# The opening of a two-block kernel on one Trainium2 core: modulation columns in four groups of 512, context prepared between the query slots

## What is computed

```python
s_lat, s_ctx = silu(c), silu(c_ctx)
mod_l = split(s_lat @ ada_w[0] + ada_b[0], 6)       # six vectors of 1024: shift, scale, gate, ...
a_lat = rmsnorm(x, norm1_g[0]) * (1 + mod_l[1]) + mod_l[0]
mod_c = split(s_ctx @ ada_w[0] + ada_b[0], 6)
a_ctx = rmsnorm(ctx, norm1_g[0]) * (1 + mod_c[1]) + mod_c[0]
p_lat = a_lat @ mix_w_in + mix_b_in                 # q, k, v and three hyena inputs
kv_ctx = a_ctx @ mix_w_in[:, KV] + mix_b_in[KV]     # k and v of the context
k_all, v_all = concat([k_c, rope(k_l)]), concat([v_c, v_l])
...                                                  # attention, hyena, out, MLP, second layer, second stack
```

## Time and profile before

| | |
|---|---|
| median of three runs | 2553.88 us |
| the profiled execution | 2555.92 us, its span 2554.1 us |
| TensorE / VectorE / ScalarE / POOL busy | 96% / 65% / 38% / 6% |
| granted TensorE clock, mean | 0.986 |
| DMA from 10 to 40 us | 393, 418 and 413 GB/s |
| loads in the queue up to q weights 0 | vec 251.5 KB, x 2 x 1024 KB, ctx 1024 KB, groups 0 to 3 of 2 x 768 KB, weights 1024 KB |
| landing of the two x halves, of ctx | 10.4 and 13.2 us, 16.2 us |
| q slot 0, q slot 1, k slot 0 on TensorE | from 47.09, 59.9 and 73.00 us |

### The profile page before, as it was taken

One profiled execution on the slowest core, in us unless ns is written; L12 is line 12 of the kernel. 1 busy time (PEld: TensorE's weight loads), 2 busy tenths in 40 slices (PEclk: granted clock), 3 DMA queues, 4 the chain that ended last, 5 costly groups with the idle time before them and its releaser, 6 DMA issues.

```text
span 2554.1 us, 27261 instructions
## 1 busy us (share of the span) xinstructions
PE 2463.0 (96%) x10726; PEld 1925.9 (75%) x10726; DVE 1662.7 (65%) x2162; ACT 960.8 (38%) x1280; POOL 162.3 (6%) x234
## 2 busy tenths in 40 slices
PE   6999879999999999999999999999999999999997
PEld 3876338788888888888766788888877667888886
DVE  7876678965668955668965695554699556733334
ACT  4325444422333422334843343122357343422221
POOL 0100140000000000000100000000001000000000
PEclk8999989999999999999999999999999999999999
DMA  7432003555552454553211234554522112223222
GB/s 289 175 125 75 17 17 107 178 190 204 171 203 91 160 178 165 181 169 120 83 57 52 74 104 163 179 181 151 179 101 92 54 44 66 85 87 118 92 86 78
DMA packets 66423, 315.36 MB, mean 123 GB/s; under 512 B 7127, under 2 KB 12631, under 8 KB 45304
## 3 DMA queue, kind: packets, MB, share of 16 engines
q1 hardware_dynamic: 41240, 222.39, 25.2%
q0 software_dynamic: 25056, 91.24, 10.9%
HBM read 311.50 MB, written 2.10 MB: 123 GB/s over the span
## 4 chain that ended last, share of the span: by engine, by line
PE 78%; DVE 12%; ACT 4%; issue 2%; DMA 2%; SPq 0%; POOL 0%; DVEq 0%; ACTq 0%
PE psum L677 20%; PE psum L678 20%; PE psum L679 20%; PE psum L1089 3%; PE psum L1045 2%; PE psum L845 2%; PE psum L1074 2%; PE psum L1063 1%; PE psum L1064 1%; DVE w_lo L1765 1%; PE psum L901 1%; DMA big<-in_ada_first 1%; DVE rstd L1608 1%; DVE squares L1654 1%; PE psum L804 1%
## 5 line engine op out<-in xcount | busy, mean ns | idle before, releaser
L1765 DVE TENSOR_TENSOR w_lo<-w_raw,w_hi 128x2048 fp32r<-128x2048 f32 (+1 forms) x192 | 418.8, 2181 | 323.7 <-ACT w_hi L1229 321.3
L677 PE MATMUL psum<-x_hi,w_hi 128*128 128x512 f32 x1568 | 618.1, 394 | 8.5 <-DVE w_lo L1765 5.3
L678 PE MATMUL psum<-x_lo,w_hi 128*128 128x512 f32 x1568 | 611.3, 390 | 0.0
L679 PE MATMUL psum<-x_hi,w_lo 128*128 128x512 f32 x1568 | 611.2, 390 | 0.0
L1229 ACT ACTIVATE w_hi<-w_raw 128x2048 fp32r<-128x2048 f32 (+1 forms) x192 | 350.5, 1826 | 505.0 <-DMA w_raw<-in_w 503.2
L678 PE MATMUL psum<-hidden_lo,w_hi 128*128 128x512 f32 x960 | 373.5, 389 | 0.0
L677 PEld LDWEIGHTS psum<-x_hi,w_hi 128*128 128x128 f32 x1568 | 295.1, 188 | 73.5 <-DVE w_lo L1765 7.2
L677 PE MATMUL psum<-hidden_hi,w_hi 128*128 128x512 f32 x896 | 349.1, 390 | 0.0
L679 PE MATMUL psum<-hidden_hi,w_lo 128*128 128x512 f32 x896 | 348.6, 389 | 0.0
L678 PEld LDWEIGHTS psum<-x_lo,w_hi 128*128 128x128 f32 x1568 | 295.2, 188 | 62.1 <-issue 3.1
L679 PEld LDWEIGHTS psum<-x_hi,w_lo 128*128 128x128 f32 x1568 | 295.0, 188 | 61.8
(11 more groups left out here) (438 smaller groups left out, 3251.4 us busy)
## 6 DMA issues: line engine op xcount, KB each, us to landing
w_raw<-in_w SPq DMA_DIRECT2D x160, 1024.0 KB, 4.9
ada_w<-in_ada POOLq DMA_DIRECT2D x168, 512.0 KB, 4.0
w_raw<-in_w SPq DMA_DIRECT2D x32, 704.0 KB, 4.1
big<-in_ada_first SPq DMA_DIRECT2D x12, 768.0 KB, 14.1
big<-in_ada POOLq DMA_DIRECT2D x6, 512.0 KB, 4.2
extra<-in_w_uq SPq DMA_DIRECT2D x8, 384.0 KB, 3.2
residual<-in_xT SPq DMA_DIRECT2D x2, 1024.0 KB, 9.4
cond_row<-in_c_row SPq DMA_DIRECT2D x4, 512.0 KB, 4.4
```

The lines of the kernel that those rows point to most:

```text
L677: mm(o, w_h, x_h, start=first, stop=False)
L678: mm(o, w_h, x_l, start=False, stop=False)
L679: return mm(o, w_l, x_h, start=False, stop=last)
L1765: v.tensor_tensor(wl[:, r, 0:n], raw[:, r, 0:n], wh[:, r, 0:n].bitcast(f32), ALU.subtract).then_inc(w_split.sem, 1)
```

## The change

Groups of 512 columns: four of them make the 2048 that are needed, in three buffers of 2 x 1 MB; the remaining columns become 32 instead of 30 (LATE_N), with 2, 2, 5, 5, 5, 5 in the slots of q, k and v. In the queue, x comes first, then the four groups, then q weights 0, ctx, q weights 1. The preparation of the context (squares, sum, root, product, modulation, high and low parts) is moved on all three engines: TensorE sums its squares between q slots 0 and 1, ScalarE evacuates q slot 0 before it takes the context's root, and VectorE starts on it after the low part of q weights 1. The low part of q weights 0 moves into `modulated`, behind the second tile. In the k slots, the context's matmuls follow all of the latent ones.

```diff
-ADA_COLS = 384
+ADA_COLS = 512
 ADA_N = 6 * D // ADA_COLS
-ADA_DEEP = 4
+ADA_DEEP = 3
+ADA_TILES = ADA_COLS // P
 CTX_ADA_N = -(-2 * D // ADA_COLS)
 
 MODS_N = 6 * D // P
 LATE_AT = CTX_ADA_N * ADA_COLS // P
 LATE_N = MODS_N - LATE_AT
-EARLY_N = 22
+EARLY_N = 24
...
-    for (i, s), count in zip(late, (2, 2, 4, 4, 5, 5, 2, 2, 2, 2)):
+    for (i, s), count in zip(late, (2, 2, 5, 5, 5, 5, 2, 2, 2, 2)):
...
-        first_norms = {T: (t1[:], rstd[:]), C: (big[:, 31, 0:C], staging[:, 0, 0:C])}
+        first_norms = {T: (t1[:], rstd[:]), C: (big[:, 31, 0:C], rstd[:, 0:C])}
...
-            load_first_ada(0)
             for half in range(2):
                 k4 = slice(4 * half, 4 * half + 4)
                 load(h[:, k4, :], a["xT"].rearrange("(k p) t -> p k t", p=P)[:, k4, :], "x_loaded%d" % half)
+            for n in range(CTX_ADA_N):
+                load_first_ada(n)
+            load_slot(mixed[0], 0)
             load(big[:, 0:4, :].rearrange("p a (b t) -> p (a b) t", t=C),
                  a["ctxT"].rearrange("(k p) t -> p k t", p=P), "ctx_loaded")
-            for n in range(1, ADA_DEEP):
-                load_first_ada(n)
-            load_slot(mixed[0], 0)
-            for n in range(ADA_DEEP, CTX_ADA_N):
-                load_first_ada(n)
             load_slot(mixed[0], 1)
             load(big[:, 28:30, :], a["rope1"].rearrange("b p t -> p b t"), "rope1_loaded")
+            load(cond_row[:], a["c_row"], "row_loaded")
             load(big[:, 30, :], a["v_bias"], "vbias_loaded")
-            load(cond_row[:], a["c_row"], "row_loaded")
             load_slot(mixed[1], 0)
...
-                            if st.name == "k":
-                                ins = three(B(4 + 2 * r + m, C), wh[:, b, w], wl[:, b, w], ch[:, k, :], cl[:, k, :], *ends)
                         if x_read and k < st.kt - 1:
                             ins.then_inc(x_read.sem, 1)
+                    if st.name == "k":
+                        for k in order:
+                            if s == 0:
+                                next_k(k)
+                            for m in range(st.mt):
+                                w = slice((k * st.mt + m) * P, (k * st.mt + m + 1) * P)
+                                ins = three(B(4 + 2 * r + m, C), wh[:, b, w], wl[:, b, w], ch[:, k, :], cl[:, k, :],
+                                            k == order[0], k == order[-1])
...
-                for t in range(3):
-                    ins = mm(ps[:, 6, 8 + 6 * n + 2 * t:10 + 6 * n + 2 * t], first_rows[:, n, t * P:(t + 1) * P],
+                for t in range(ADA_TILES):
+                    at = 8 + 2 * (ADA_TILES * n + t)
+                    ins = mm(ps[:, 6, at:at + 2], first_rows[:, n, t * P:(t + 1) * P],
                              V("group_sum", 0, 2), start=True, stop=True)
...
             first_ada(0)
             first_sum_of(T)
-            first_ada(1)
-            first_sum_of(C)
-            turn(0)
-            for n in range(2, CTX_ADA_N):
+            for n in range(1, CTX_ADA_N):
                 first_ada(n)
                 turn(n - 1)
             me.count(turn(CTX_ADA_N - 1).then_inc(S("ada_turned").sem, 1), S("ada_turned"))
-            products(mixed[0], xh, xl)
-            products(mixed[1], xh, xl)
+            slot(mixed[0], 0, xh, xl, next_k)
+            first_sum_of(C)
+            slot(mixed[0], 1, xh, xl)
+            products(mixed[1], xh, xl, False)
             products(mixed[2], xh, xl, False)
...
-            first_squares([ctx_in[:, k, :] for k in range(KD)], C, KD - 1, {0: "ctx_loaded"})
             first_scale(T, 6, 1)
-            row_copy(0)
-            first_scale(C, 7, 2)
-            for n in range(1, ADA_DEEP):
+            for n in range(CTX_ADA_N):
                 row_copy(n)
             split_hi(0)
-            for n in range(ADA_DEEP, CTX_ADA_N):
-                row_copy(n)
             norm_his([xh[:, k, :] for k in range(KD)], [xz[:, k, :] for k in range(KD)])
             split_hi(1)
+            first_squares([ctx_in[:, k, :] for k in range(KD)], C, KD - 1, {0: "ctx_loaded"})
+
+            ident_f = ACT.Identity
+
+            def q_out(s, o, r, dst):
+                return act(dst, B(2 * r + o), ident_f, bias=q_bias[:, 2 * s + o:2 * s + o + 1], scale=64 ** -0.5)
+
+            evacuate(mixed[0], 0, q_out)
+            first_scale(C, 7, 2)
             norm_his([ch[:, k, :] for k in range(KD)], [cz[:, k, :] for k in range(KD)])
             row_sigmoid(1)
-
-            ident_f = ACT.Identity
-            stage(mixed[0], lambda s, o, r, dst: act(dst, B(2 * r + o), ident_f, bias=q_bias[:, 2 * s + o:2 * s + o + 1],
-                                                     scale=64 ** -0.5))
+            evacuate(mixed[0], 1, q_out)
...
-            def modulated(tiles, g, shift, x_h, x_l):
+            def modulated(tiles, g, shift, x_h, x_l, weights=None):
...
                     eng.wait_ge(*me.own())
+                    if k == 1 and weights is not None:
+                        split_lo(weights)
                     if k >= 1:
                         low(k - 1)
...
             summed(KD, T)
+            normed(h_tiles, T, x_mod)
+            eng.wait_ge(S("ada_turned").sem, S("ada_turned").next(me))
+            turned = ps[:, 6, 8:8 + 2 * LATE_AT].rearrange("p (m b) -> p m b", b=2)
+            me.count(v.tensor_tensor(mods[:, 0, 0:LATE_AT], turned[:, :, 0], V("ada_b0", 0, LATE_AT), ALU.add).then_inc(me.done.sem, 1), me.done)
+            eng.wait_ge(*me.own())
+            gains(gain[:, :], mods[:, 0, 8:16], V("norm1_g0", 0, 8))
+            modulated(x_mod, gain, mods[:, 0, 0:8], x_hi, x_lo, 0)
+            split_lo(1)
             summed(KD, C)
-            normed(h_tiles, T, x_mod)
             normed([ctx_in[:, k, :] for k in range(KD)], C, ctx_mod)
-            split_lo(0)
-            eng.wait_ge(S("ada_turned").sem, S("ada_turned").next(me))
-            turned = ps[:, 6, 8:8 + 6 * CTX_ADA_N].rearrange("p (m b) -> p m b", b=2)
-            me.count(v.tensor_tensor(mods[:, 0, 0:3 * CTX_ADA_N], turned[:, :, 0], V("ada_b0", 0, 3 * CTX_ADA_N), ALU.add).then_inc(me.done.sem, 1), me.done)
-            eng.wait_ge(*me.own())
-            gains(gain[:, :], mods[:, 0, 8:16], V("norm1_g0", 0, 8))
-            modulated(x_mod, gain, mods[:, 0, 0:8], x_hi, x_lo)
-            split_lo(1)
-            me.count(v.tensor_tensor(modc[:], turned[:, :, 1], V("ada_b0", 0, 3 * CTX_ADA_N), ALU.add).then_inc(me.done.sem, 1), me.done)
+            me.count(v.tensor_tensor(modc[:], turned[:, :, 1], V("ada_b0", 0, LATE_AT), ALU.add).then_inc(me.done.sem, 1), me.done)
             eng.wait_ge(*me.own())
             gains(gainc[:, :], modc[:, 8:16], V("norm1_g0", 0, 8))
             modulated(ctx_mod, gainc, modc[:, 0:8], [ch[:, k, :] for k in range(KD)], [cl[:, k, :] for k in range(KD)])
```

More of the change, by code:

```diff
@@ L229, in build @@
         mods = place("mods", [P, 2, 48])
-        modc = place("mods_ctx", [P, 3 * CTX_ADA_N])
+        modc = place("mods_ctx", [P, LATE_AT])
         sc = place("sig_c", [P, 16])
@@ L2000, in _ @@
             summed(KD, T)
-            summed(KD, C)
             normed(h_tiles, T, x_mod)
-            normed([ctx_in[:, k, :] for k in range(KD)], C, ctx_mod)
-            split_lo(0)
             eng.wait_ge(S("ada_turned").sem, S("ada_turned").next(me))
-            turned = ps[:, 6, 8:8 + 6 * CTX_ADA_N].rearrange("p (m b) -> p m b", b=2)
-            me.count(v.tensor_tensor(mods[:, 0, 0:3 * CTX_ADA_N], turned[:, :, 0], V("ada_b0", 0, 3 * CTX_ADA_N), ALU.add).then_inc(me.done.sem, 1), me.done)
+            turned = ps[:, 6, 8:8 + 2 * LATE_AT].rearrange("p (m b) -> p m b", b=2)
+            me.count(v.tensor_tensor(mods[:, 0, 0:LATE_AT], turned[:, :, 0], V("ada_b0", 0, LATE_AT), ALU.add).then_inc(me.done.sem, 1), me.done)
             eng.wait_ge(*me.own())
             gains(gain[:, :], mods[:, 0, 8:16], V("norm1_g0", 0, 8))
-            modulated(x_mod, gain, mods[:, 0, 0:8], x_hi, x_lo)
+            modulated(x_mod, gain, mods[:, 0, 0:8], x_hi, x_lo, 0)
             split_lo(1)
-            me.count(v.tensor_tensor(modc[:], turned[:, :, 1], V("ada_b0", 0, 3 * CTX_ADA_N), ALU.add).then_inc(me.done.sem, 1), me.done)
+            summed(KD, C)
+            normed([ctx_in[:, k, :] for k in range(KD)], C, ctx_mod)
+            me.count(v.tensor_tensor(modc[:], turned[:, :, 1], V("ada_b0", 0, LATE_AT), ALU.add).then_inc(me.done.sem, 1), me.done)
             eng.wait_ge(*me.own())
```

## The result

The changed kernel takes 2564.84 us (median of five runs, 2558.01 to 2565.92); the kernel before took 2553.88 (2552.97 to 2556.68). The ratio over all runs is 1.0032, 95% interval 1.0021 to 1.0044: slower by 0.32%, which on 2553.88 us is 8.2 us. The profiled execution took 2565.53 us with a span of 2563.7, so 9.6 us above that of before, at a mean granted clock of 0.984 against 0.986.

A forecast was written before the change was run, and what follows sets the result against it. TensorE is busy for 96%, but VectorE bounds the stretch from mods to k slot 0. Terms -7.5 + 12.7 + 2.6 = +7.8 us took the median from 2553.88 to 2561.7; 8 in 10: 2556 to 2567, own range 2559 to 2564.

The forecast's parts named there:

- When the columns are ready: Opening: turned modulation columns reach VectorE at 37.0 us instead of 44.52, -7.5 us (ends -9.5 and -6.4).
- The chain: VectorE's serial work from mods to the end of split_lo(2) grows from 28.5 us by +12.7 (12.0 to 13.4).
- k slot 0: VectorE releases TensorE's first k weight slot at 78.2 us, 5.2 us later than before.
- The two stops of TensorE: TensorE idles twice: about 3 us between the q slots and over 7 us before k slot 0.
- The late columns: k and v slots: two added modulation columns and their load waits on VectorE cost +2.6 us, bounds 0 and 4.6.
- The rest: Work behind 200 us is the same and shifts as a whole, 0 us.
- (a): Rival: context preparation fits beside the q slots, TensorE is the bound; faster, 2547.2 us; chance 0.07.
- (b): Rival: small loss, clock whole at group 3 (mods at 35.0), no late-column cost; +3.2 us, 2557; chance 0.20.
- (c): Rival: half clock from group 3 to the last turn, mods at 38.1, columns 3.6; +9.9 us, 2563.8; chance 0.23.
- (d): The likeliest case for the whole kernel: 2558.9 to 2563.5 us; chance 0.50.
- Ahead of its first product it mostly waits for the loads: Opening before the change: TensorE's waits ahead of its first product are mostly for modulation group loads; no size given.

The follow-up runs named there:

- experiment 2: The changed kernel with two late modulation columns left out and set to zero (30 late columns as before); ratio 1.0033 to the kernel before.
- experiment 3: The changed kernel with three places for all 24 early columns, instead of two from column 18 on; ratio 1.002 to the kernel before.
- experiment 4: The changed kernel with the context's root ahead of q slot 0's evacuation on ScalarE; ratio 1.0047 to the kernel before.
- experiment 9: The changed kernel with split_lo(2) moved from the end of VectorE's chain into its wait for the context's root; ratio 1.004 to the kernel before.
- experiment 10: The changed kernel with three places for early columns, context's root ahead of q's evacuation, and split_lo(2) behind the context's products; ratio 1.0024 to the kernel before.
- experiment 1: The changed kernel with the context's squares, sum, root and product in their old place and its load right behind x; ratio 1.0035 to the kernel before.
- experiment 5: The changed kernel with the context prepared in its old place and three places for the early columns; ratio 0.9992 to the kernel before.

## Why the prediction was right, and which term was mis-sized

Forecast were 2561.7 us and slower. The measured median is 2564.84, inside the range for 8 in 10 (2556 to 2567) and 0.8 above the forecast's own range (2559 to 2564); the ratio, which rests on both kernels' runs, gives 2562.1. That the sum came so near is in part luck: the start was 1.85 us better and the columns 3.8 us worse than forecast, and the two partly cancelled (+9.6 in the profile for +7.8).

- **When the columns are ready, -7.5.** Measured -9.35. Group 3 was there at 29.88 at the latest, 0.8 before the 30.7 of the queue's arithmetic, and the clock cost 1.4 us at group 3 but nothing at the last two turns. Over the six profiles that share this opening (changed, 2 to 4, 9, 10) mods came at 33.9 to 36.2: I took a point (37.0) later than all of them. The Trainium skill ("TensorE: Matmul & The Clock Gate", section "HAM oscillation — how this bites in real kernels") describes a throttle that comes back at every wait for DMA between bursts of 16 matmuls; the waits it tells of last about 3 to 5 us, those here 0.4 to 2.9. Taken for these gaps too, as the prediction took it, it gives a start at 38.1. The trace agrees only in part: in each of the six profiles at least one of groups 2 and 3 was slow (2.61 to 3.60 us), but in three of them the other ran at 1.90, and the last 16 matmuls of the turns took 1.95 to 2.10 us in all.
- **The chain, +12.7.** Measured +12.30, term by term: first product 4.62 us behind mods (4.6), split_lo(0) +2.0 (2.1; by experiment 1), sum 3.36 and its copy 0.15 (3.5), root wait 2.63 (3.1), reciprocal and products 4.5 (4.5), the 0.55 us wait for the high part gone. Experiment 1 shows 10.3 us of it by undoing them, experiment 4 the root wait by itself.
- **k slot 0.** Predicted 5.2 us later (78.2), measured 2.94 (75.94): 1.85 of the 2.3 by the earlier mods, 0.4 by the shorter chain. The two stops of TensorE came with the forecast sizes, 2.9 and 7.3 us.
- **The late columns, +2.6, at most 4.6.** Measured +6.43: this is the step that failed, in size and in its upper bound. The mechanism was as named, up to v1's evacuations: VectorE reached them 3.2 us later than before relative to the chain's end (149.51 - 75.89 against 143.41 - 72.94; 2.6 forecast). I then let v1's own five columns keep their length. From the evacuations to the maxima went 22.85 us, before 19.57: 3.3 us more: column 20's load was issued only behind the weight load at 146.26 and took 7.7 us, and column 23's took 6.1. The forecast priced each load at the 3.88 us of a load with no weight load close ahead of it. Experiment 2 shows in the profile that without the two columns all of it goes. A third place takes 7.6 us off too, but 5.1 of them also in the old order; with three places in both the two columns cost 3.9 us, inside the forecast's bound of 4.6.
- **The rest, 0.** Measured +0.22.
- **The rivals.** (a) fell with the chain's 40.7 us. (b) had the start nearly right (35.0), but by luck: the clock was not whole at group 3, the group came earlier than reckoned; and it had no late columns. (c) named the sum (+9.9; 9.6 in the profile) for the wrong reasons: the clock was not slow in full; the columns were dearer than its 3.6. The likeliest case (d), 2558.9 to 2563.5, holds the ratio's 2562.1 and not the median.
- **A reading that was off, without weight in the sum.** "Ahead of its first product it mostly waits for the loads": of the 20.9 us of waits from 0 to 47 us in the view of the earlier trace rows, 9.7 are for loads and 11.2 for VectorE (6.7 ahead of `first_sum_of` and 4.5 ahead of the very first matmuls).

What stays open: the 1.4 us by which the profile of the changed kernel (+9.6) exceeds the ratio's 8.2 are within what single executions differ by. And the order of the ratios does not follow the first maxima everywhere: experiment 5 has its maxima 2.2 us behind those of experiment 3 and the lower ratio, with intervals that don't touch (up to 1.0003, from 1.0011); experiment 2 has its maxima 5.1 us ahead of the changed kernel's and the same ratio. I did not settle why the context's old place is worth more in time than at the maxima. One candidate is the clock that an execution gets. The eleven executions of experiment 5 run from 2543.06 us at a mean granted clock of 0.990 to 2556.92 at 0.986, with a mean of 0.9874, where those of experiment 3 have 0.9859; and in the profile of the kernel before the mean clock is 0.93 up to 180 us, 0.96 from there to 600 us and 1.00 behind. Whether the clock makes the time or follows from it, no run here separates. How near column loads and weight loads may come was read from loads that happened to fall so, and not tried by moving one load alone.

## What to carry to other kernels

Work that stood in an engine's waiting time cost nothing here, and it cost its full length once it was moved behind the event that the engine waited for: an earlier start has to be weighed against all that then becomes serial. Here 9.35 us of earlier start cost 12.3 us of chain. And when an engine that feeds itself from few buffers gets more items, price the loads' issue and their neighbours in the queue, not the items alone: in the profiles two columns of 1.3 us cost 6.4 us, and 3.9 with one more buffer in both orders. And test the cure on the old kernel as well: the third buffer was the one edit that made a kernel faster than before, and it needed nothing of the change.

## What the runs showed of the hardware that was not expected

- A 512 KB load took 3.9 us from issue to landing when no weight load was close ahead of it (the one at 147.81 of the kernel before), and 7.6 and 6.0 us when a 1 MB load had been issued 1.3 and 2.1 us ahead on the other queue; in experiment 5 it took 7.7 us with the 1 MB load issued 0.7 us behind it. Over all thirteen profiles it is 4.7 to 9.1 us within 2.2 us behind a weight load and a median of 4.4 us clear of one. Two queues do not keep loads apart.
- The same opening fell into different clocks. Rows of TensorE's timeline, experiment 10 and then experiment 9:

```profile
25.00 1.90 PE L725 MATMUL psum<-big,silu_c 128*2 128x512 f32 x16 [2.10 <-DMA big<-in_ada_first]
26.83 1.05 PE L734 MATMUL psum<-vec,first_rows 128*128 128x2 f32 x8
29.97 3.39 PE L725 MATMUL psum<-big,silu_c 128*2 128x512 f32 x16 [2.09 <-DMA big<-in_ada_first]
...
25.33 3.56 PE L725 MATMUL psum<-big,silu_c 128*2 128x512 f32 x16 [2.81 <-DMA big<-in_ada_first]
...
30.30 1.90 PE L725 MATMUL psum<-big,silu_c 128*2 128x512 f32 x16 [0.42 <-DMA big<-in_ada_first]
```

  In experiment 10 group 2 ran at the whole clock (1.90 us) behind 2.10 us of idling and group 3 at about half (3.39) behind 2.09. In experiment 9 it was the other way round: group 2 took 3.56 us behind 2.81 and group 3 1.90 behind 0.42. The idle time just before a group does not by itself say at which clock it runs, and mods moves by 2.3 us with it: over the six profiles it stands at 33.93 and 34.18 where group 3 took 1.90 us, and at 35.17 to 36.22 where it took 3.31 to 3.59.
